# The last feed-forward block (512 tokens) in the seven-product form

## The reference

```python
for l in range(DEPTH):                       # DEPTH = 2
    need_ctx = l < DEPTH - 1
    h = h + 0.5 * m[:, 2] * swiglu(modulate(h, m[:, 0], m[:, 1]), w_ff1_in[l], w_ff1_out[l])
    hc = hc + 0.5 * mc[2] * swiglu(modulate(hc, mc[0], mc[1]), w_ff1_in[l], w_ff1_out[l])
    ...                                      # mixer: h = h + m[:, 5] * y
    h = h + 0.5 * m[:, 8] * swiglu(modulate(h, m[:, 6], m[:, 7]), w_ff2_in[l], w_ff2_out[l])
    if need_ctx:
        hc = hc + mc[5] * yc
        hc = hc + 0.5 * mc[8] * swiglu(modulate(hc, mc[6], mc[7]), w_ff2_in[l], w_ff2_out[l])

def swiglu(t, w_in, w_out):
    gate, up = jnp.split(t @ w_in, 2, axis=-1)
    return (jax.nn.silu(gate) * up) @ w_out
```

## Time and profile before

| | us |
|---|---|
| median of the runs (3) | 3274.56 |
| lowest and highest | 3272.66, 3278.45 |
| the profiled execution, its own time | 3272.6 |
| its span in the trace | 3270.8 |
| TensorE busy | 3102.8 (95%) |
| VectorE busy | 1938.7 (59%) |
| ScalarE busy | 1110.4 (34%) |
| first matmul of block 3 to its last | 2899.19 to about 3261.4 |

### The profile page before, as it was taken

One profiled execution on the slowest core, in us unless ns is written; L12 is line 12 of the kernel. 1 busy time (PEld: TensorE's weight loads), 2 busy tenths in 40 slices (PEclk: granted clock), 3 DMA queues, 4 the chain that ended last, 5 costly groups with the idle time before them and its releaser, 6 DMA issues.

```text
span 3270.8 us, 43730 instructions
## 1 busy us (share of the span) xinstructions
PE 3102.8 (95%) x17735; PEld 2739.3 (84%) x17735; DVE 1938.7 (59%) x2755; ACT 1110.4 (34%) x1734; POOL 266.0 (8%) x317
## 2 busy tenths in 40 slices
PE   5999999999999998898999999999999998999999
PEld 4999999987669895488999988999998876678887
DVE  7754536524552536757778765877778548643333
ACT  4211212356441321235323334532323436632222
POOL 1100000200001005620000001000000100000000
PEclk8999999999999999999999999999999999999999
DMA  6533424411004220012343321333333120023332
GB/s 209 169 102 108 124 72 137 127 36 52 7 1 129 59 64 14 1 39 70 112 129 104 116 65 59 110 97 102 111 116 110 56 61 8 14 83 97 96 97 90
DMA packets 314304, 274.20 MB, mean 84 GB/s; under 512 B 17426, under 2 KB 290057, under 8 KB 313865
## 3 DMA queue, kind: packets, MB, share of 16 engines
q1 hardware_dynamic: 286992, 182.35, 18.7%
q0 software_dynamic: 25488, 89.14, 8.7%
q10 hardware_dynamic: 1641, 0.14, 0.0%
HBM read 263.21 MB, written 8.39 MB: 83 GB/s over the span
## 4 chain that ended last, share of the span: by engine, by line
PE 50%; DVE 4%; ACT 2%; issue 1%; POOL 0%; ACTq 0%; DVEq 0%
PE ps L2236 28%; PE ps L497 16%; PE ps L1453 1%; DVE hs_lo L2437 1%; ACT gpt L1492 1%; DVE vw_lo L2169 1%; ACT gp L1505 1%; PE ps L1211 1%; PE ps L1477 1%; PE ps L1435 1%; PE ps L2318 0%; DVE ms_s L2468 0%; DVE h_sb L2445 0%; PE ps L1891 0%; PE ps L1908 0%
## 5 line engine op out<-in xcount | busy, mean ns | idle before, releaser
L487 DVE TENSOR_TENSOR w_lo<-ring,w_hi 128x1024 fp32r<-128x1024 f32 (+3 forms) x221 | 251.4, 1139 | 450.2 <-ACT w_hi L472 361.7
L497 PE MATMUL ps<-u_hi,w_hi 128*128 128x384 f32 (+2 forms) x1584 | 469.1, 356 | 19.6 <-DVE u_lo L663 15.4
L497 PE MATMUL ps<-u_lo,w_hi 128*128 128x384 f32 (+2 forms) x1584 | 461.9, 351 | 0.0
L497 PE MATMUL ps<-u_hi,w_lo 128*128 128x384 f32 (+2 forms) x1584 | 461.5, 351 | 0.0
L472 ACT CAST w_hi<-ring 128x1024 fp32r<-128x1024 f32 (+3 forms) x157 | 149.4, 952 | 612.3 <-PE ps L497 574.1
L497 PEld LDWEIGHTS ps<-u_hi,w_hi 128*128 128x128 f32 x1584 | 284.9, 190 | 47.9 <-issue 23.2
L497 PEld LDWEIGHTS ps<-u_lo,w_hi 128*128 128x128 f32 x1584 | 286.4, 190 | 22.7 <-issue 1.7
L2169 DVE TENSOR_TENSOR vw_lo<-ring,vw_hi 128x1024 fp32r<-128x1024 f32 (+1 forms) x176 | 211.2, 1200 | 155.6 <-ACT vw_hi L2163 155.3
L497 PEld LDWEIGHTS ps<-u_hi,w_lo 128*128 128x128 f32 x1584 | 285.4, 189 | 21.2
L2163 ACT CAST vw_hi<-ring 128x1024 fp32r<-128x1024 f32 (+1 forms) x176 | 181.3, 1030 | 330.5 <-PE ps L2236 267.4
L2236 PE MATMUL ps<-u_hi,vw_hi 128*128 128x384 f32 x768 | 249.0, 338 | 11.8 <-DVE u_lo L663 10.9
(11 more groups left out here) (350 smaller groups left out, 5854.8 us busy)
## 6 DMA issues: line engine op xcount, KB each, us to landing
ring<-in_w_ff_in SPq DMA_DIRECT2D x176, 512.0 KB, 4.0
ring<-in_w_ff_out SPq DMA_DIRECT2D x72, 512.0 KB, 4.0
cst<-in_w_mod POOLq DMA_DIRECT2D x72, 512.0 KB, 3.9
m_in<-in_w_mod POOLq DMA_DIRECT2D x56, 512.0 KB, 4.0
ring<-in_w_in_e SPq DMA_DIRECT2D x26, 512.0 KB, 3.9
m_first<-in_w_mod POOLq DMA_DIRECT2D x16, 512.0 KB, 13.9
ring<-in_w_out_e SPq DMA_DIRECT2D x16, 512.0 KB, 3.8
ring<-in_w_ff_out SPq DMA_DIRECT2D x16, 384.0 KB, 3.4
```

What stands on the lines that cost most here:

```text
L487: dve.tensor_tensor(w_lo[:, b:b + WIDE[n]], ring[:, s:s + WIDE[n]], w_hi[:, b:b + WIDE[n]], ALU.subtract).then_inc(w_split_lo, 1)
L497: mm = pe.matmul(ps_at(p, c0, c1) if halved else pair(p)[:, c0:c1], w, x[:, c0:c1], start=start and i == 0, stop=stop and i == 2)
```

## The change

Block 3 is put into the seven-product form: `STR` becomes (1, 2, 3), and the calls of `sync_ff`, `act_ff`, `pe_ff`, `dve_ff` for block 3 become those of the `_s_` functions, with waits at the end of the program moved to their semaphores. With 512 tokens a half is 256 tokens, so A and P chunks have matmuls of 256 columns; O chunks have 512. It has no modulation items.

The plan `S_MODS` is touched as well: the result of a job is now written in the slot in which PE makes it (two chunks after the fold), no longer one later, and the next job starts there. The tables `urgent` and the other `usual` apply to block 0, which isn't in `STR`.

```diff
-STR = (1, 2)
+STR = (1, 2, 3)
...
+            urgent = {...} if i_f == 0 else {}
+            usual = {2: 2, 3: 2, 4: 1, 6: 1} if i_f == 0 else {2: 1, 3: 2, 4: 1}
             for c, ch in enumerate(S_ORDER[i_f]):
-                cap = {2: 1, 3: 2, 4: 1}.get(ch[2], 0) if ch[0] == "A" else 3
-                if ch[0] == "P":
-                    cap = 0
+                cap = 3 if ch[0] == "O" else usual.get(ch[2], 0) if ch[0] == "A" else 0
...
-                if busy >= 0 and c == busy + 2:
+                if busy >= 0 and c == busy + (3 if urgent and done == jobs[0] else 2):
                     plan[c]["pe"].append(done)
-                if busy >= 0 and c == busy + 3:
                     plan[c]["dve"].append(("d", done))
                     busy = -1
...
-                back_to_back = i_f - 1 in STR and i_f > 1
+                back_to_back = i_f == 2 and 1 in STR
...
-            sync_ff(f, 3)
+            sync_s(f, 3)
...
-            pe_ff(pe, 3)
+            pe_s_ff(pe, 3)
...
-                        pe.wait_ge(o_res, RES[R_FF(3, 2)] + d + 1)
+                        pe.wait_ge(o_res, RES[R_FF(3, LAST(3))] + d + 1)
...
-            act_ff(act, 3)
+            act_s_ff(act, 3)
...
-                act.wait_ge(w_used, n_)
+                act.wait_ge(o_mm, DB * len(SPART) * len(STR))
...
-            dve_ff(dve, 3)
+            dve_s_ff(dve, 3)
+            dve_s_residual(dve, 3, len(SPART) - 1, DB - 2)
+            dve_s_residual(dve, 3, len(SPART) - 1, DB - 1)
```

More of the change, by code:

```diff
@@ L2088, in build @@
                 todo += [("p", x, k, first + k, s) for k in range(DB) for s in range(2)] + [("f", x)]
-            plan, c = {}, 0
+            plan = {}
             busy = -1
+            urgent = {("P", 0, 0): 3, ("P", 0, 1): 3, ("P", 0, 2): 2, ("P", 0, 3): 1, ("A", 1, 0): 1, ("A", 1, 1): 1,
+                      ("A", 1, 2): 1, ("A", 1, 3): 2, ("A", 1, 4): 2, ("A", 1, 5): 1} if i_f == 0 else {}
+            usual = {2: 2, 3: 2, 4: 1, 6: 1} if i_f == 0 else {2: 1, 3: 2, 4: 1}
             for c, ch in enumerate(S_ORDER[i_f]):
-                cap = {2: 1, 3: 2, 4: 1}.get(ch[2], 0) if ch[0] == "A" else 3
-                if ch[0] == "P":
-                    cap = 0
+                cap = 3 if ch[0] == "O" else usual.get(ch[2], 0) if ch[0] == "A" else 0
+                if urgent and ch[0] != "O" and ch[1] < 2:
+                    cap = urgent.get(ch, 0)
                 plan[c] = {"dve": [], "pe": []}
-                if busy >= 0 and c == busy + 2:
+                if busy >= 0 and c == busy + (3 if urgent and done == jobs[0] else 2):
                     plan[c]["pe"].append(done)
-                if busy >= 0 and c == busy + 3:
                     plan[c]["dve"].append(("d", done))
```

## The result

| | before | after |
|---|---|---|
| median of the runs, us | 3275.76 (4 runs) | 3332.06 (4 runs) |
| lowest and highest | 3272.66, 3278.45 | 3329.12, 3332.90 |
| span of the profiled execution | 3270.8 | 3331.1 |
| its mean granted clock | 0.982 | 0.976 |

The changed kernel is slower: the ratio is 1.0173, with a 95% interval of 1.0157 to 1.0189. That is 56 us in the medians and 60.3 us between the two profiled spans. The forecast was +34.8 us; its sign was right, and 3332 lies above its range.

A forecast was written before the change was run, and what follows sets the result against it. PE was taken as the bound. Block 3: 344.4 work + 1.5 slow start + 47.7 waits = 393.6 against 362.2, +31.4; with the plan's +3.4, 3274.6 + 34.8 = 3309 us, range 3288 to 3326.

The forecast's parts named there:

- restarts: Block 3: the first matmuls after a wait run longer; about 31 restarts at 0.1 us each, 3 us.
- first body (A2, A3, A4): Block 3's first body: mixing occupies DVE, so PE waits 1.7, 1.1 and 3.8 us at these chunks, 6.6 us.
- A4 of first bodies after O (5): Block 3, first body after O chunks: copy due at 11.5, ready at 12.65; 1.15 us five times, 5.8 us.
- A0 and load, second bodies (4): Block 3, second bodies: 0.8 us waiting for a product, about 0.5 for the last weight load, four times.
- A4, second bodies: Block 3, second bodies: PE waits 2.1 us for ACT's copy queued behind a waiting cast, in four bodies.
- entries of O chunks, four blocks: Block 3, five parts: third and fourth hidden blocks ready late; 1.9 us once, 2.3 four times, 11.1 us.
- two-block part: Block 3: 3.2 us at the entry, then 0.85, 1.8, 1.8 for residuals behind rests awaiting casts; 7.6 us.
- rival 3: PE's waits drop the clock to 1.2 GHz, 17 us a body; one or two drops, 3315 to 3330 us; 6%.
- Rival 1: ACT and DVE keep ahead in block 3: 13.3 us less there, with the plan 3265 us; 4%.
- 2 (waits half as large): Block 3: ACT and DVE overlap more of their start-up; +7.7 us, with the plan +11, 3286 us; 9%.
- Rival 4: Block 3: two weight loads at once take 6.5 us and bound it; 2.6 us more in four bodies, 3320; 8%.
- The plan: Blocks 1 and 2: moved modulation items make PE late by 0.7 us at four third O chunks; +3.4 us total, 0 to 6.

The follow-up runs named there:

- block3_only: The changed kernel with the modulation plan as it was before, so only block 3 differs from before: 3323.07 us, ratio 1.0150.
- plan_only: The kernel before with the new plan for the modulation items alone: 3284.15 us against 3274.18, ratio 1.0031.
- all orders: Changed kernel, old plan; in block 3 copies before casts, addition and residuals before rests, sum 1 behind products: 3294.73 us, ratio 1.0082.
- the experiment: Changed kernel, but in block 3 sum 1 behind the first body adds an already landed weight tile (computation altered): 3324.97 us, ratio 1.0143.
- before_planned: Kernel before, blocks 1 and 2: residuals ahead of rests, copy ahead of cast in first body only, merged plan with other caps: 3255.58 us, ratio 0.9952.
- the fillers: Changed kernel with extra 256-column matmuls into unread banks ahead of PE's waits at A4 and A0 in block 3: 3323.95 us, ratio 1.0139.

## Why the prediction was wrong in size

Three terms of the sum for block 3 failed. The 1.5 us at 1.2 GHz were 13.4; the residuals in the O chunks of four-block parts, put at nothing, were 7.3 (5.2 of it idle time); and the restarts were 11.8 instead of 3 (0.16 us in each of 44 waits, 7.1 together, and the 4.7 of "rest"). The idle time in front of the waits, 44.7 forecast, came to 42.2. The steps, losses by the start-to-start count (us), where each wait has its 0.16 in it:

| step | forecast | measured |
|---|---|---|
| PE's work | 344.4 | 344.3 |
| first body (A2, A3, A4) | 6.6 | 5.7 (0.87, 1.11, 3.71) |
| A4 of first bodies after O (5) | 5.8 | 6.3 |
| A0 and load, second bodies (4) | 5.2 | 9.7 |
| A4, second bodies | 8.4 | 4.0 |
| entries of O chunks, four blocks | 11.1 | 9.8 |
| two-block part | 7.6 | 6.6 |
| residuals in four-block O chunks | 0 | 7.3 |
| restarts | 3 | 4.7 (rest) |
| at 1.2 GHz | 1.5 | 13.4 |

**Right.** The work, to 0.1 us; the trace's spacing of 0.120 and 0.227 held, and with it the 15.0 us of saving. The waits in sum, with restarts: 47.7 forecast, 54.0 found. That they come so close is in part luck: 5.2 us of idle time for residuals and 8.8 of restarts that the forecast lacked were offset by 7.6 us less idle time in the other steps. The mechanism at A4, with the copy behind the cast for A5 as in the earlier trace rows, was shown by taking it away. The five waits after O chunks measured 1.10 to 1.11 us idle and 0.16 for the restart, the forecast said 1.15 (its own terms, 2.3 and 10.2 against 11.5, give 1.0). From A4 to A4 of the one pair of bodies without a stretch at 1.2 GHz between them (3075.83 to 3099.73) are 23.9 us; the forecast's period was 23.1 and 0.5 for the load. The four new waits in third O chunks came at the four places (0.83, 1.14, 0.98 and 1.13 idle), larger than 0.7.

**Wrong: the clock (rival 3).** This is the largest error: 11.9 us in block 3 and 4.1 in blocks 1 and 2, of 25.5 us missing in the profiled spans; the stage between, with 2.0 us more, may add to it. I gave the rival 6%, wrote that 0.50 is read only behind the norm (the trace of before has it at 1711, 2162, 2448 and 2537 too), and argued from one stretch of the earlier trace rows, where the clock stayed at 1.00 in spite of waits. In the changed kernel just there, behind waits of the same size, stood two stretches at 1.2 GHz. One stretch could not show that it does not happen. The view that could have was on hand: 0.99 and 0.98 granted over blocks 1 and 2 of before. Of the 12.0 us that this is by the count, 6.5 are four stretches at 1.2 GHz away from the blocks' starts, beside 27 waits. An estimate from these numbers, one such stretch for every 7 waits and 1.5 us for each, gives 6.6 us on the 31 waits that the forecast counted and 9.4 on the 44 that came, and would have brought the upper end of the range to the result; it says nothing of the cause, and those four stretches did not stand behind waits. I also took the rival as an alternative to the forecast, when it comes on top of the waits that the forecast itself announced, and priced it wrongly: one or two drops of up to 17 us each, where there were seven stretches of 1.5 to 2.6 us. Its own marker (a granted clock below 0.95 in block 3) was set too low: 0.96 over 412 us is enough for 12 us.

The two don't simply add. While PE is slow, DVE and ACT catch up: in the three second bodies with a stretch at 1.2 GHz behind A0 the wait at A4 is 0.51 to 0.53 us, in the one without it is 1.80. That is why A4 came out at half of my 2.1 us. And `block3_only`, with 7.4 us at 1.2 GHz, has 51.2 us of waits against 49.3.

The untouched stage took 304.5 us before, 303.2 in `plan_only`, 304.6 in `block3_only` and 306.4 after, with the granted clock at 0.965 before and 0.957 after, which is 2.7 us more lost. I put its 2 us down to chance of the clock, not to the change; that is argued, not shown.

**Wrong: residuals in O chunks.** I followed the odd residual only in the two-block part. Its path (PE done, cast 1.05, rest 1.14, residual 0.75, together some 3.2 us with the hand-overs) has to be set against one output tile, which is 12 x 0.227 = 2.7 us in a four-block part, not against the chunk of 5.45 us. In the trace the second to fourth O chunk of a part begin with this (three in each of the first four such parts, one in the last, 13 in all):

```profile
2975.04 0.50 PE L2238 MATMUL ps<-hs_hi,vw_hi 128*128 128x512 f32 x1 [0.40 <-DVE h_sb L2447]
2981.19 0.50 PE L2238 MATMUL ps<-hs_hi,vw_hi 128*128 128x512 f32 x1 [0.40 <-DVE h_sb L2447]
2987.34 0.50 PE L2238 MATMUL ps<-hs_hi,vw_hi 128*128 128x512 f32 x1 [0.40 <-DVE h_sb L2447]
```

The starts are 6.15 us apart instead of 5.45. At 768 tokens the same residual was hidden, so nothing in the rows of before showed it; the sum of the queue did.

**Wrong in place: second bodies.** Forecast 13.6 us, measured 13.7, but for the wrong reasons: the load (0.5 a body taken, 1.5 found in DVE's waits) and the order at A0 took what A4 gave back.

**The other rivals.** Rival 1 (the saving arrives) and 2 (waits half as large) found nothing: even with all orders mended the waits are 26.9 us. Rival 4's marker was met (DVE waited over 1 us ahead of sum 1 in three of four bodies), but the experiment prices it at about 1 us a body, not 2.6.

**The plan.** Forecast 3.4 us (0 to 6), measured 10 (6 to 14). The four waits were each up to 0.4 us larger than taken; the rest goes with the mean clock of the runs.

## What stays open

What brings the clock down in blocks 1 and 2 is not settled. Before, at 1711 and 2162, PE ran at 1.2 GHz in the middle of chunks of 384 columns, with no wait for some 50 us ahead of it (1660.81 and 2111.68 are the last); `before_planned`, with hardly a wait for residuals or copies left, still has five such stretches in these blocks. In block 3 of before, 360 us of 512-column matmuls have none behind the start, and in block 3 after all but the start follow a wait. In blocks 1 and 2 after, away from the blocks' starts, three of seven stretches begin within 1.5 us of the end of a wait (2099.50, 2472.07, 2491.52), the other four do not. So the waits are shown as the cause in block 3 (by the fillers), but not in blocks 1 and 2. Nor is it known why the same wait is followed by 1.2 GHz in one place or execution and not in another.

## What to carry to other kernels

When a change makes PE's pieces shorter and leaves the side engines' pieces as they are, follow each in-order queue through one whole period against the smallest unit of PE's work that waits for it, and book each wait with its restart and a share of 1.2 GHz behind it; what the granted clock of a long stretch lacks to 1, times its length, gives that share at most. An instruction that somebody waits for should not stand behind one that waits itself, but where a chain sets the period, mending one place only moves the wait: mend the places together and read the waits' sum, not the row. A fault found in the new code may stand in the old one too: part of the same reordering and a plan around it made the kernel before 17 us faster, while the changed block, 29.4 us shorter with all orders, was still slower than the plain one.
